# Compression of the cached rows in three rounded passes, and norm chains in another order

## What is computed

```python
def compress_kv(rows, pe, w1, w2):      # rows (B, L, 2, G, dh)
    ch = rows.reshape(B, n_ch, CMP_STRIDE, 2, G, dh)       # chunks of 16 rows
    pre = einsum('cld,clde->ce', pe, w1)                   # position part, the same for all blocks
    for m in range(2):                                     # two taps: a block of 32 rows is two chunks
        pre = pre + einsum('bnlcgd,clde->bncge', ch[:, m:m + n_c], w1c[:, m])
    return einsum('bncge,ced->bncgd', gelu(pre), w2)
```

## Time and profile before

| what | us |
| --- | --- |
| median of 3 runs (lowest, highest) | 1352.21 (1348.97, 1356.15) |
| profiled execution, its time | 1352.22 |
| its span | 1350.4 |
| PE busy | 1321.9 (98%) |
| DVE busy | 783.4 (58%) |
| ACT busy | 550.8 (41%) |
| POOL busy | 122.2 (9%) |

### The profile page before, as it was taken

One profiled execution on the slowest core, in us unless ns is written; L12 is line 12 of the kernel. 1 busy time (PEld: TensorE's weight loads), 2 busy tenths in 40 slices (PEclk: granted clock), 3 DMA queues, 4 the chain that ended last, 5 costly groups with the idle time before them and its releaser, 6 DMA issues.

```text
span 1350.4 us, 26246 instructions
## 1 busy us (share of the span) xinstructions
PE 1321.9 (98%) x10344; PEld 1223.8 (91%) x10344; DVE 783.4 (58%) x1625; ACT 550.8 (41%) x1085; POOL 122.2 (9%) x136
## 2 busy tenths in 40 slices
PE   7999999999999999999999999999999999999996
PEld 5789888999999979999898687899899999999996
DVE  1238786789622344446456645554599888973333
ACT  1145454566412133223236455532566555652111
POOL 3010000000011120000003110043300000001110
PEclk9999999999999999999999999999999999999998
DMA  9942777322344346354572220073132223323331
GB/s 343 321 140 63 281 255 252 117 96 95 119 154 153 91 157 193 116 179 137 157 252 79 93 94 17 25 214 110 45 95 94 95 94 100 120 81 93 86 85 66
DMA packets 97712, 180.84 MB, mean 134 GB/s; under 512 B 13973, under 2 KB 47381, under 8 KB 96446
## 3 DMA queue, kind: packets, MB, share of 16 engines
q1 hardware_dynamic: 88678, 163.81, 37.4%
q10 hardware_dynamic: 8920, 15.46, 3.2%
HBM read 173.11 MB, written 10.28 MB: 136 GB/s over the span
## 4 chain that ended last, share of the span: by engine, by line
PE 94%; DVE 3%; DMA 1%; ACT 1%; issue 1%; SPq 0%; POOL 0%; ACTq 0%; POOLq 0%; DVEq 0%
PE PS L2208 36%; PE PS L2273 32%; PE PS L2553 7%; PE PS L2094 4%; PE PS L2229 3%; PE PS L2157 2%; PE PS L2567 2%; PE PS L2579 2%; PE PS L2595 2%; PE PS L2112 1%; PE PS L2494 1%; PE PS L2176 1%; DMA ch<-in_cmp_pages 1%; DVE wl L1448 0%; PE PS L2461 0%
## 5 line engine op out<-in xcount | busy, mean ns | idle before, releaser
L2273 PE MATMUL PS<-X,wh 128*128 128x272 f32 x2240 | 428.1, 290 | 0.5 <-issue 0.4
L2273 PEld LDWEIGHTS PS<-X,wh 128*128 128x128 f32 x2240 | 351.7, 188 | 15.4 <-issue 11.8
L2273 PE MATMUL PS<-X,wl 128*128 128x272 f32 x1120 | 323.5, 289 | 0.0
L1448 DVE TENSOR_TENSOR wl<-raw,wh 128x1024 fp32r<-128x1024 f32 (+3 forms) x131 | 138.4, 1057 | 256.2 <-ACT wh L1013 256.0
L1013 ACT ACTIVATE wh<-raw 128x1024 fp32r<-128x1024 f32 (+3 forms) x129 | 113.3, 879 | 361.8 <-PE PS L2208 337.8
L2273 PEld LDWEIGHTS PS<-X,wl 128*128 128x128 f32 x1120 | 210.7, 188 | 0.0
L2208 PE MATMUL PS<-hl,wh 128*128 128x272 f32 x704 | 145.2, 288 | 0.0
L1074 ACT ACTIVATE wh<-S 128x512 fp32r<-128x512 f32 x160 | 100.5, 628 | 63.1 <-DVE S L1556 33.5
L1537 DVE TENSOR_TENSOR wl<-S,wh 128x512 fp32r<-128x512 f32 x160 | 109.9, 687 | 26.9 <-ACT wh L1074 26.7
L2208 PEld LDWEIGHTS PS<-hl,wh 128*128 128x128 f32 x704 | 110.5, 188 | 0.0
L2208 PE MATMUL PS<-X,wh 128*128 128x272 f32 x544 | 107.4, 288 | 0.0
(11 more groups left out here) (313 smaller groups left out, 2274.0 us busy)
## 6 DMA issues: line engine op xcount, KB each, us to landing
raw<-in_w_gu SPq DMA_DIRECT2D x88, 512.0 KB, 4.2
ada<-in_w_ada SPq DMA_DIRECT2D x24, 1024.0 KB, 5.4
raw<-in_w_in SPq DMA_DIRECT2D x39, 512.0 KB, 4.4
raw<-in_w_dn SPq DMA_DIRECT2D x32, 384.0 KB, 3.2
raw<-in_w_dn SPq DMA_DIRECT2D x32, 320.0 KB, 2.9
ada<-in_w_ada ACTq DMA_DIRECT2D x8, 1024.0 KB, 13.7
ch<-in_cmp_pages SPq DMA_DIRECT2D x56, 128.0 KB, 6.7
kv<-in_sel_pages SPq DMA_DIRECT2D x112, 64.0 KB, 2.0
```

The costliest lines, as they stand in the source:

```text
L1448: e.tensor_tensor(wl[:, u % SPLITS, 0:n, :], raw[:, u % RAWS, 0:n, :], f(wh[:, u % SPLITS, 0:n, :]), ALU.subtract).then_inc(lo_ready, 1)
L2273: ins = mm(triple(i, PASS_BANK[j]), w[:, k, :], X[:, s, part, k, :], start=(j in (A11, A12, S1) and k == 0 and w is wh_ and part == 0), st ...
```

## The change

It does these things:

- Weights `w1` and the cached rows are split: ACT rounds them (`cache_weight_rounded(c)`, `cache_rounded(p)` in two halves of pages), DVE takes the remainders (`cache_weight_lo(c)`, `cache_low(p)`) in place over the raw data. `compress(p)` becomes 48 rounded products, and `compress_first` 32 of 128 columns and 32 of 256.
- The two taps go into two halves of a PSUM bank. DVE copies one and adds the other, shifted by one chunk, into `hid` (`cache_sum(p)`), and `cache_hidden` works in `hid`.
- `position_bias` is cut into c = 0, ahead of `compress_first`, and c = 1, behind it. The ada steps of the head come later in PE's list, and ACT's and DVE's lists are woven anew. `hank` lies elsewhere and is loaded once `pre_ready` is 8.
- Norms: `norm_spread` and the diagonal go in two halves with a semaphore step each, `scaled(0)` too, also for the final output; ACT rounds key tile 0 before it modulates tile 1; `two_units` starts key tile 0 with the products that need only `u_hi`; ada steps of norm 1 are 0, 1, 4 before its last sums, 2, 3 behind them and 5, 6, 7 behind the spread (before: 0, 1 / 2, 3, 4 / 5, 6, 7, as norm 2 still has); in `down1` the last `lo` goes behind the last residual.

```diff
+            def cache_weight_rounded(c):
+                e.wait_ge((comp_in, comp1_in)[c], 16)
+                e.activation((w1_0hi, w1_1hi)[c][:, :, :], (w1_0, w1_1)[c][:, :, :], ACT.Copy).then_inc(cache_w_hi, 1)
+            def cache_rounded(p):
+                t, c = divmod(p, 2)
+                if CACHE_HI_FREE[p]:
+                    e.wait_ge(pre_ready, CACHE_HI_FREE[p])
+                for b in range(2):
+                    js = slice(NPG * b, NPG * b + NPG)
+                    ...
+                    e.activation(cache_hi(p)[:, js].rearrange("p j l g n -> p j l (g n)"),
+                                 cache_rows(t)[:, js, :, c, :, :].rearrange("p j l g n -> p j l (g n)"),
+                                 ACT.Copy).then_inc(cache_hi_ready, 1)
+            cache_weight_rounded(0)
+            cache_rounded(0)
...
-            e.wait_ge(ch_second_in, 16 * NPG)
             for half in range(2):
                 ks = slice(4 * half, 4 * half + 4)
                 e.dma_start(h[:, ks, :], d["xT"][:, ks, :]).then_inc(x_in[half], 16)
-            for k in range(4):
-                ada0_load(k)
+            cache_weight_rounded(1)
+            cache_rounded(1)
+            ada0_load(0)
+            ada0_load(1)
             cache_hidden(0)
+            cache_rounded(2)
+            ada0_load(2)
+            ada0_load(3)
             e.wait_ge(x_in[1], 16)
             for k in range(4, KD):
                 e.activation(normed(0, k), h[:, k, :], ACT.Square).then_inc(x_sq, 1)
+            cache_rounded(3)
             cache_hidden(1)
+            cache_hidden(2)
             ada0_load(4)
-            cache_hidden(2)
+            root(0)
+            cache_rounded(4)
+            cache_hidden(3)
             ada0_load(5)
-            root(0)
-            cache_hidden(3)
             ada0_load(6)
+            cache_rounded(5)
+            cache_hidden(4)
             ada0_load(7)
-            cache_hidden(4)
+            cache_rounded(6)
             cache_hidden(5)
+            cache_rounded(7)
             split(0)
             split(1)
             norm(0)
...
             def position_bias():
-                e.wait_ge(pe_part, 1)
+                cache_weight_lo(0)
+                cache_low(0)
+                e.wait_ge(pe_part, 2)
                 e.tensor_copy(part0[:, 0:2 * P], PS[:, PE_BANK, 0:2 * P]).then_inc(pe_kept, 1)
+                cache_weight_lo(1)
                 e.wait_ge(pe_ready, 1)
                 e.tensor_copy(peb[:, :], PS[:, PE_BANK, 2 * P:2 * P + 2]).then_inc(pe_copied, 1)
...
             position_bias()
+            cache_low(1)
+            cache_sum(0)
+            cache_low(2)
+            cache_sum(1)
...
+            position_bias(0)
             compress_first()
-            position_bias()
-            compress(1, range(0, 4))
+            position_bias(1)
+            compress(1, range(0, 16))
             e.wait_ge(csil_ready, 1)
             e.wait_ge(consts_in, 16)
             position_total()
-            compress(1, range(4, 16))
+            compress(1, range(16, 48))
+            compress(2)
             ada_step(0)
-            compress(2)
-            ada_step(1)
             compressed(0)
             norm_sum(0)
-            compress(3, range(0, 8))
+            compress(3, range(0, 24))
             norm_spread(0)
-            compress(3, range(8, 16))
+            compress(3, range(24, 48))
+            ada_step(1)
             ada_step(2)
-            ada_step(3)
...
```

More of the change, by code:

```diff
@@ L1487, in norm @@
                     cache_keys(0)
+                    cache_low(5)
+                    cache_sum(4)
                     cache_keys(1)
+                    cache_low(6)
+                    cache_sum(5)
+                    cache_low(7)
                     lo(0)
@@ L2060, in _, with position_bias @@
                 mm(PS[0:NH, 2 + c % 2, 0:b - a], relx[:, :], oneh[:, a:b], start=True, stop=True).then_inc(f_ready, 1)
[L2062 to L2072, removed]
+            def position_bias(c):
+                e.wait_ge((comp_in, comp1_in)[c], 16)
+                if c == 0:
+                    e.wait_ge(pad_zero, 1)
+                    e.wait_ge(vec_in, 16)
+                for kt in range(16):
+                    q = kt % 4
+                    ins = mm(PS[32 * q:32 * q + 32, PE_BANK, P * c:P * c + P],
+                             vec[:, V_PE + 16 * c + kt:V_PE + 16 * c + kt + 32], (w1_0, w1_1)[c][:, kt, :],
+                             start=kt < 4, stop=kt >= 12, skip_group_check=True)
                 ins.then_inc(pe_part, 1)
@@ L2081, in position_total, with cache_product @@
                 ins.then_inc(pe_ready, 1)
[L2083 to L2091, removed]
-                for x in products:
-                    m, lp = divmod(x, 8)
-                    ins = mm(PS[:, 4 + p % 2, 1 - m:257 - m].rearrange("p (g j n) -> p g j n", g=2, n=8),
-                             (w1_0, w1_1)[c][:, 8 * m + lp, :],
-                             cache_rows(t)[:, :, lp, c, :, :].rearrange("p j g n -> p g j n"),
-                             start=(x == 0), stop=(x == 15), skip_group_check=True)
-                if products[-1] == 15:
+            def cache_product(p, x, js=slice(0, 2 * NPG)):
+                c = p % 2
+                part, y = divmod(x, 16)
+                m, lp = divmod(y, 8)
+                rows = cache_lo(p)[:, js, lp, :, :] if part == 1 else cache_hi(p)[:, js, lp, :, :]
+                w = ((w1_0lo, w1_1lo) if part == 2 else (w1_0hi, w1_1hi))[c]
+                return mm(PS[:, 4 + p % 2, 256 * m:256 * m + 256].rearrange("p (g j n) -> p g j n", g=2, n=8)[:, :, js],
+                          w[:, 8 * m + lp, :], rows.rearrange("p j g n -> p g j n"),
+                          start=(x == 0 and js.start == 0), stop=(x == 47), skip_group_check=True)
@@ L2223, in two_units @@
                         e.wait_ge(lo_ready, u + 2)
+                    hi_first = k == 0 and ready[0] is u_lo
                     if v == 0:
-                        e.wait_ge(ready[0], ready[1] + k + 1)
+                        e.wait_ge(u_hi if hi_first else ready[0], ready[1] + k + 1)
                     o = out2(slots[v])
+                    if hi_first:
+                        for w in (wh, wl):
+                            for a in range(2):
+                                mm(o[:, a, :], w[:, (u + v) % SPLITS, 0, :], xh(0, a), start=(w is wh), stop=False)
+                        if v:
+                            e.wait_ge(u_lo, ready[1] + 1)
+                            for y in range(2):
+                                for a in range(2):
+                                    mm(out2(slots[y])[:, a, :], wh[:, (u + y) % SPLITS, 0, :], xl(0, a), start=False, stop=False)
+                        continue
                     for w, x in ((wh, xh), (wh, xl), (wl, xh)):
```

166 lines of the change are left out of this document (128 added, 38 removed).

## The result

| | before | after |
| --- | --- | --- |
| median us, 16 runs each (lowest, highest) | 1353.03 (1348.97, 1358.93) | 1360.47 (1356.57, 1363.73) |
| profiled execution, its time (span) | 1352.22 (1350.4) | 1360.84 (1359.0) |
| first FFN unit starts | 90.96 | 103.75 |
| from there to the sums of norm 1 | 396.2 | 397.1 |
| sums of norm 1 to those of norm 2 | 466.4 | 463.8 |

The ratio after to before is 1.0051, 95% interval [1.004, 1.0063]. The forecast was 1351.9 with a range of 1342 to 1359; the time lies 8.6 us above the one and 1.5 above the other. The lower rows of the table are starts of matmuls in the two traces: the head lost 12.8 us (forecast: 3.3), the rest gained 4.2 (forecast: 3.6).

A forecast was written before the change was run, and what follows sets the result against it. TensorE, busy 98% of the span, was taken as the bound. Head waits of 13.8 us against 10.5 saved gave +3.3, norms -3.6, so 1352.2 became 1351.9 us; range 1342 to 1359.

The forecast's parts named there:

- Products, -9.0: Compression, seven positions: 32 products at 219 ns become 48 rounded ones at 119 ns, 49.0 to 40.0 us.
- Position 0, -1.5: First compression position: 9.68 us before; after, 32 half-width and 32 full products, 7.6 us plus 0.6 for the slow start.
- Wait for position 1's remainder, +6.5: Head: PE waits from 30.7 to 37.2 us for cache_low(1) on DVE, slowed by GpSimd; 3.2 without that neighbour.
- hi(2), +1.4: Head: PE, ready at 41.0 us, waits for ACT's cache_rounded(2) until 42.4, behind cache_sum(0), table load and Gelu.
- the remainder of position 0, +0.3: Head: PE ends its half-width products by 23.3 us and waits for DVE's cache_low(0) until 23.6.
- Start, +2.85 and +0.95: Head: position_bias(0) waits for vec until 16.8 us, not 13.95 (+2.85); its half runs at 1.2 GHz (+0.95).
- From there the lists run ahead of PE.: Head after position 2's rounding: positions 3, 4, 5 have their halves 1 to 3 us early; no wait until the turn.
- Turn, +1.8: Head's end, at ada_step(7)/ada_turn(0): PE waits 1.8 us for DVE's queued remainders and keep_part(0) behind ACT's rounding and splits.
- the one on the slower side: Rival: DVE bounds the head because remainders read short strided runs and take half as long again; 1360 us, chance 0.12.
- if the waits lie after 50 us: Sign that the forecast is wrong: PE's waits in the head fall later than 50 us.
- if the spacing is outside 112 to 126: Sign that the forecast is wrong: compression matmuls, expected 119 ns apart, are spaced outside 112 to 126 ns.
- Norm 2: Second norm after the head: halves and hi_first give -0.4 us (0 to -0.8); the earlier diagonal gives nothing.

The follow-up runs named there:

- norms alone: The kernel before with only the norm edits, the compression as it was: 1348.59 us, ratio 0.9965 to the kernel before.
- the products by themselves: The kernel after with seven loops of unread rounded products, of several widths and layouts, appended behind the last norm: 1424.33 us in one run.
- pages early: The kernel after with the last two page loads released earlier and half the last load issued from ACT's queue: 1356.05 us, ratio 1.0023 to before.
- the remainder first: The kernel after with cache_low(1) moved on DVE ahead of the wait for the position part's second half: 1356.02 us, ratio 1.0021 to before.
- the last two kernels: The kernel after with five head edits, rounded rows laid near included (1346.34 us, 0.9953), then also ada0_load(1) issued later (1345.53 us, 0.9937).
- the four repairs together: The kernel after with full-width position 0, cache_low(1) sooner, earlier page loads and vec loaded sooner: 1348.33 us, ratio 0.9971 to before.
- the near layout: The kernel after with the rounded cached rows laid in runs 16 elements apart instead of 128: 1360.1 us, ratio 1.0052 to before.
- the head alone: The kernel after with the norm edits taken back, leaving the rounded compression, its lists and hank: 1364.65 us, ratio 1.0084 to before.

## Why the prediction was wrong

The bound and the norms were right. PE sets the end, and the earlier trace rows led to the right place. Norms: forecast -3.6, measured -4.7 [-6.8, -2.7] alone; from norm 1's sums to the end it is -5.1 in after's trace and -3.4 in that of the norms alone. Norm 1 was put at -2.5 and the stretch that holds it is 2.6 shorter in after, norm 3 at -0.7 for 0.5.

The head was put at +3.3 and is +12.8. By the terms of the sum:

- **Products, -9.0 (119 ns).** Mis-sized, the largest miss beside position 0. At 134 ns seven positions gain 7 x 48 x 15 = 5.0 us less, outside the bounds of 112 to 125.5. (At 125.5 the saving would be 49.0 - 42.2 = 6.8, not the 8.0 in the forecast.) They were taken from products that stream adjacent columns and scaled by the number of columns. That the layout costs 15 to 18 ns is shown by the products by themselves and in place, and the chain of the head could not have given it.
- **Position 0, -1.5 (8.2 us).** This step failed. It took 13.24, 5.0 more: 0.6 was allowed for a slow start, but all 32 half-width products and 24 of the others ran at the pace of 1.2 GHz (213 to 220 ns). Before, the low pace lasted 4.6 us, and I carried that length over to products of another kind. Full-width ones take back 3.9 of position 0.
- **Wait for position 1's remainder, +6.5.** Place, releaser and queue were right, the size was not: 3.1 us, since the slow position 0 brought DVE to it at 33.2 in place of 28.8 us, when POOL was nearly done. The low clock behind the wait was put at about 1, which the sum left out; it took 26 products at some 85 ns more, 2.2 us. Together 5.3 for the 6.5 of the sum.
- **hi(2), +1.4, and the remainder of position 0, +0.3.** Not there: PE came later than planned. **Start, +2.85 and +0.95**: right (16.63 us; 1.93 for the half, of which 0.94 is the doubled part).
- **"From there the lists run ahead of PE."** This step had the wrong path. The lists do; the pages don't. I followed ACT's and DVE's order, but not that SP's page loads wait for `pre_ready`, which the longer position 0 and 1 push back by 8 us. In after's trace that is 2.6 us of waiting at position 6 and 1.4 at the low clock behind it, 4.0 in all and none of it in the sum; pages early gives back 3.8 by the ratios.
- **Turn, +1.8**: 1.3 to 1.6 in after, by the queue that was named; 2.1 to 2.9 in the traces where the pages cost less at position 6 or landed latest.
- **Before, at nothing.** The forecast took 219 ns for all seven positions, from one clean stretch, so 49.0 us. The pieces of before's chain for them (L2094) add up to 51.6. Most of the rest is 16 records behind the first norm's sums:

```profile
45.16 5.39 PE L2094 MATMUL PS<-ch,w 128*128 128x256 f32 x16
```

```profile
47.00:49.00 2.00, 2.00 (x6) 0.50 1.06 392
```

(timeline of PE; window of PE alone). They take 5.23 us from start to start, the next 16 take 3.55: 1.7 us of low clock that before's execution paid and after's, at 1.00 behind the same sums, did not. It comes and goes: norms alone, the remainder first, the added products and the last two kernels have it, the others don't.

The differences sum to 5.0 + 5.0 - 1.2 - 1.7 + 4.0 - 0.3 = 10.8, in the order of the list; without the 1.7 us of low clock that before paid, 9.1. The head missed by 9.5.

In the trace the four repairs together take 14.4 us off the head, more than the 12.8 lost; one of them (vec early, not run by itself) also takes away part of the +3.8 that was forecast.

Of the rivals, the one on the slower side had the right sign by the wrong mechanism: DVE's 1024-element remainders take 1.22 us, as the long runs of the earlier trace rows do; the short runs cost DVE nothing here. Short runs far apart cost PE. Of the signs of being wrong, "if the waits lie after 50 us" and "if the spacing is outside 112 to 126" named two of the failures; none named position 0.

**Norm 2** was -0.4 and the trace has -2.0. That is mostly not the change: the stretch behind it took 381.6 with the same edits in the norms alone. The windows of 12 us from its first sum, in the norms-alone kernel and in after (PE alone counted):

```profile
949.30:961.30 12.00, 11.77 (x97) 0.72 0.16 45
```

```profile
964.70:976.70 12.00, 10.23 (x108) 1.00 0.14 44
```

The execution with the granted clock at 0.72 has the stretch of 381.6 us, the one at 1.00 has 378.9; before had 0.86 and 381.0. One trace cannot price such a term.

## What to carry to other kernels

When work moves to a new form of instruction, look not only at its width and type in the nearest row but at how its operand lies, and time that form by itself: 15 ns on each of 336 products, 5 us, was half of the 10.5 us planned. A change that delays one engine delays every transfer that waits for its semaphore, so follow each wait of the load queues too, not only the lists of the computing engines. Mend waits together: each single mend showed the next one, and one (the near layout) gained nothing by itself. And when a term of the kernel before is scaled up from its cleanest stretch, add up the whole stretch as well: here that hid 2.6 us.

## What the runs showed of the hardware

- A rounded product of 256 columns with a new weight tile: 118 ns with runs of 8 elements 16 apart, 120 side by side, 135 with runs of 8 elements 128 apart; 272 columns side by side 125; 128 columns 110, all at the full clock. At 0.50: 216 for 128 columns, 220 for 256.
- 96 products of 128 columns back to back, 21 us, left the granted clock at 0.50; 128 of them, 14 us, begun at 1.00 left it at 1.00.
- Behind the one-column sums of the first norm the granted clock was 0.50 in the kernel before (47 to 49 us) and 1.00 in after (55 to 57 us); of twelve traces six show the low level there.
- SP took 10.0 to 10.5 us to issue the 16 DMAs of the last pages; the last of them landed 5.7 us after that in the head alone and 8.7 in after, with the same list.
- DVE's two-input subtraction of 1024 elements took 2.15 us beside GpSimd's operations and 1.22 without; GpSimd's add of 544 went from 1.35 to 3.26 us at the same time.
